# Hybrid SSD/attention/mLSTM/MoE block on one core: two parameter queues, a reordered first norm, and modulation columns by narrow matmuls

## The reference

```python
h = rmsnorm(x, norm_mix) * (1 + scale) + shift
x = x + gate * mixer(h)
h = rmsnorm(x, norm_ffn) * (1 + scale_f) + shift_f
x = x + gate_f * moe(h)
```

## Time and profile before

| | |
|---|---|
| median of 3 runs | 1325.04 us (1325.0 to 1326.84) |
| the profiled execution's own time | 1311.33 us |
| its span | 1309.5 us |
| TensorE busy | 1105.2 us, 84% |
| VectorE, ScalarE, GpSimd busy | 39%, 19%, 17% |
| mean granted TensorE clock | 0.912 of full speed |

### The profile page before, as it was taken

One profiled execution on the slowest core, in us unless ns is written; L12 is line 12 of the kernel. 1 busy time (PEld: TensorE's weight loads), 2 busy tenths in 40 slices (PEclk: granted clock), 3 DMA queues, 4 the chain that ended last, 5 costly groups with the idle time before them and its releaser, 6 DMA issues.

```text
span 1309.5 us, 13521 instructions
## 1 busy us (share of the span) xinstructions
PE 1105.2 (84%) x5097; PEld 576.4 (44%) x5097; DVE 510.6 (39%) x1004; ACT 249.0 (19%) x481; POOL 224.4 (17%) x218
## 2 busy tenths in 40 slices
PE   3899978799899479999999199998868489869992
PEld 0445444443454434444455164445544355434441
DVE  0434656655501522221222678326461433322213
ACT  2222121365511400000001332111010301000001
POOL 0001031000011063333211302000001174332001
PEclk8899978899999789999999599999668789999997
DMA  9732155779161359999995832122007279999982
GB/s 354 224 106 89 66 192 193 249 260 392 63 257 67 130 197 408 409 416 415 347 400 231 330 124 69 64 102 92 1 0 321 100 270 411 413 416 417 425 333 111
DMA packets 74366, 309.79 MB, mean 237 GB/s; under 512 B 11789, under 2 KB 14013, under 8 KB 57131
## 3 DMA queue, kind: packets, MB, share of 16 engines
q1 hardware_dynamic: 63947, 292.70, 57.4%
q0 software_dynamic: 9472, 12.77, 2.8%
q10 hardware_dynamic: 864, 3.15, 0.6%
HBM read 308.41 MB, written 15.34 MB: 247 GB/s over the span
## 4 chain that ended last, share of the span: by engine, by line
PE 70%; DMA 10%; DVE 10%; ACT 3%; issue 3%; SPq 3%; POOL 1%; ACTq 0%; POOLq 0%; DVEq 0%
PE psum L1828 9%; DMA arena<-in_moe_w 9%; PE psum L1831 9%; PE psum L1196 7%; PE psum L1101 6%; PE psum L1863 5%; PE psum L551 5%; PE psum L1858 4%; PE psum L543 3%; PE psum L1209 2%; PE psum L377 2%; SPq L2023 2%; PE psum L996 2%; PE psum L1447 1%; PE psum L838 1%
## 5 line engine op out<-in xcount | busy, mean ns | idle before, releaser
L1944 POOL DMA_INDIRECT arena<-hdram,idxl x128 | 128.7, 1005 | 258.1 <-DVE arena L1903 168.7
L1918 DVE TENSOR_TENSOR arena<-arena,psum 128x512 f32<-128x512 f32 x32 | 22.0, 687 | 271.7 <-PE psum L1828 142.4
L1196 PE MATMUL psum<-arena,ring 128*128 128x512 f32 (+1 forms) x256 | 97.8, 540 | 0.0
L1828 PE MATMUL psum<-arena 128*64 128x256 f32 x736 | 82.8, 381 | 8.8 <-DMA arena<-in_moe_w 7.4
L1831 PE MATMUL psum<-ring,arena 128*128 128x512 f32 x176 | 78.9, 606 | 10.6 <-DVE arena L1903 9.8
L1828 PE MATMUL psum<-ring,arena 128*64 128x256 f32 x672 | 77.7, 389 | 11.6 <-DVE arena L1903 9.2
L1101 PE MATMUL psum<-ring,arena 128*128 128x512 f32 x192 | 82.9, 593 | 1.5 <-ACT arena L1086 1.5
L1125 POOL TENSOR_TENSOR xres<-xres,arena 128x512 f32<-128x512 f32 x12 | 15.2, 1262 | 384.2 <-DVE arena L1114 384.2
L1886 ACT ACTIVATE arena<-psum 128x512 f32<-128x512 f32 x32 | 19.1, 597 | 281.7 <-PE psum L1858 173.7
L1903 DVE STREAM_TRANSPOSE arena<-arena 128x1024 f32<-128x1024 f32 x32 | 64.9, 2029 | 18.3 <-DMA arena<-hdram,idxl 18.3
L551 PE MATMUL psum<-ring,arena 128*128 128x512 f32 (+1 forms) x192 | 69.0, 522 | 0.0
(11 more groups left out here) (369 smaller groups left out, 1572.6 us busy)
## 6 DMA issues: line engine op xcount, KB each, us to landing
ring<-in_moe_w SPq DMA_DIRECT2D x48, 2048.0 KB, 14.4
arena<-in_moe_w SPq DMA_DIRECT2D x48, 2048.0 KB, 15.5
ring<-in_w_mod SPq DMA_DIRECT2D x24, 2048.0 KB, 8.9
ring<-in_od_w_in SPq DMA_DIRECT2D x6, 2048.0 KB, 11.3
ring<-in_ev_w_in SPq DMA_DIRECT2D x3, 2048.0 KB, 9.2
arena<-ydram SPq DMA_DIRECT2D x6, 1024.0 KB, 6.9
ring<-in_ev_w_out SPq DMA_DIRECT2D x2, 2048.0 KB, 12.5
ring<-in_od_w_out SPq DMA_DIRECT2D x2, 2048.0 KB, 7.7
```

The costliest lines, as they stand in the source:

```text
L1196: mm = pe.matmul(bank(bk, tok.stop - tok.start), w[:, k, P * (b % 4):P * (b % 4) + P], hT[:, k, tok], start=k == 0, stop=k == KD - 1)
L1828: mm = pe.matmul(psum[64 * g:64 * g + 64, hbank(e, j), 0:256], xT[b][:, k, 0:64], w[:, k, 256 * g:256 * g + 256], start=k == 0, stop=k == ...
L1944: pool.indirect_dma_start(xq[e % NX][:, 256 * g:256 * g + 256], None, xrows(l), bass.IndirectOffsetOnAxis(ap=idxl[:, g, e:e + 1], axis=0), ...
```

## The change

Seven parameters (convolution weights and biases, norm weights, `b_mod`) stay in SyncE's queue. The other 17 (`LATER`) are issued by GpSimd once the memory is cleared and chunk 1's rows are done; a second semaphore counts them. The steps that need them, `act_setup_rest` and a new `dve_setup_later`, are moved behind the xBC evacuations and convolutions. The first half of the first norm's transposes is put ahead of chunk 3 in TensorE's program. Chunk columns are made by a float32 matmul with a 128x2 selector, `streamsel`, which transposes, picks and sums in one; the result is 8 columns in bank 7, copied by VectorE, and the next chunk's rows wait for that copy. In the rounds for long lists TensorE's four semaphores become one.

```diff
+    streamsel = cf[:, 618:620]
...
     PARAMS = [
-        (cb[:, :], const_b),
         (r3[0:18, :], ev_conv_w[0].rearrange("t (b n) -> (t b) n", n=P)),
...
         (brow[0:2 * MODC, :], b_mod.rearrange("l (c n) -> (l c) n", n=512)),
+    ]
+    LATER = [
+        (cb[:, :], const_b),
         (rw32[:, :, 0:E], router_w.rearrange("(k p) e -> p k e", p=P)),
...
-            PARAMS.append((rowpar[r:r + H, j:j + 1], w[0, d].unsqueeze(1)))
+            LATER.append((rowpar[r:r + H, j:j + 1], w[0, d].unsqueeze(1)))
...
     def act_setup_rest():
-        act.wait_ge(S("params"), PARAMS_IN)
+        act.wait_ge(S("later"), LATER_IN)
...
         dve.wait_ge(*dve_more("cols_ready"))
+
+    def dve_setup_later():
+        dve.wait_ge(S("later"), LATER_IN)
         dve.wait_ge(*dve_more("c_exp"))
...
     def pe_mod_rows(m):
+        if m > 0:
+            pe.wait_ge(S("mcol_done"), m)
         weights_here(mod_pos(m))
...
     def pe_mod_cols(m):
         pe.wait_ge(*pe_more("modrow_ready"))
-        if m > 0:
-            pe.wait_ge(*pe_more("mcol_done"))
         for b in range(4):
-            mm = pe.transpose(psum[:, 6, P * b:P * b + P], modrow[:, P * b:P * b + P], ident)
+            mm = pe.matmul(psum[:, 7, 2 * b:2 * b + 2], modrow[:, P * b:P * b + P], streamsel, start=True, stop=True)
...
-        dve.tensor_reduce(mcol[:, l, 4 * ch:4 * ch + 4, :],
-                          bank(6).rearrange("p (b g r) -> p b r g", b=4, g=4)[:, :, 0:2, :], AX.X, ALU.add
-                          ).then_inc(S("mcol_done"), 1)
+        dve.tensor_copy(mcol[:, l, 4 * ch:4 * ch + 4, :], bank(7, 8).rearrange("p (b r) -> p b r", b=4)
+                        ).then_inc(S("mcol_done"), 1)
...
     def pe_norm(tiles):
-        pe.wait_ge(*pe_more("xn_ready", len(tiles)))
-        for k in range(KD):
+        pe_norm_blocks(tiles, range(4))
+        pe_norm_blocks(tiles, range(4, KD))
+
+    def pe_norm_blocks(tiles, blocks):
+        if blocks[0] == 0:
+            pe.wait_ge(*pe_more("xn_ready", len(tiles)))
+        for k in blocks:
...
     def pe_router(l, tiles):
-        pe.wait_ge(S("params"), PARAMS_IN)
+        pe.wait_ge(S("later"), LATER_IN)
...
+    def pool_later():
+        pool.wait_ge(S("zeroed"), 1)
+        pool.wait_ge(S("mod_full"), 2)
+        for dst, src in LATER:
+            pool.dma_start(dst, src).then_inc(S("later"), 16)
...
         def _(eng):
+            pool_later()
             pool.wait_ge(S("in_full"), 4)
...
             act_mod(3)
-            act_setup_rest()
             act_norm_rows(0, 0, ALL)
             act.wait_ge(*act_more("raw_cleared"))
             act_in_even("xbc")
+            act_setup_rest()
             act_conv()
...
             dve_mod(2)
+            dve_setup_rest()
             dve_mod(3)
-            dve_setup_rest()
...
-            for m in range(FIRST):
+            for m in range(FIRST - 1):
                 pe_mod(m)
             pe_setup_rest()
-            pe_norm(ALL)
+            pe_norm_blocks(ALL, range(4))
+            pe_mod(FIRST - 1)
+            pe_norm_blocks(ALL, range(4, KD))
             pe_in_even()
...
+    f[:, 618:620] = np.arange(P)[:, None] % DIR1 == np.arange(2)
```

More of the change, by code:

```diff
@@ L316, in hybrid_program @@
             r = DIR1 * d + (2 * DIR1 if w is od_fgate_b else 0)
-            PARAMS.append((rowpar[r:r + H, j:j + 1], w[0, d].unsqueeze(1)))
+            LATER.append((rowpar[r:r + H, j:j + 1], w[0, d].unsqueeze(1)))
     PARAMS_IN = 16 * len(PARAMS)
+    LATER_IN = 16 * len(LATER)
     def act_setup():
@@ L509, in pe_norm @@
             mm.then_inc(S("ht_full"), 1)
-        pe.wait_ge(*pe_more("ht_act", 2))
-        pe.wait_ge(*pe_more("ht_dve", 2))
+        if blocks[0] > 0:
+            pe.wait_ge(*pe_more("ht_act", 2))
+            pe.wait_ge(*pe_more("ht_dve", 2))
     EV0 = FIRST
@@ L593, in dve_in_even @@
                      colsa[:, 66 + b:67 + b])
+        dve_setup_later()
         dve.wait_ge(S("in_full"), 7)
@@ L2056, in body @@
         def body(r, e, n):
-            turn, last = sp.to_reg(n + 6), sp.to_reg(n + 1)
+            turn, last = sp.to_reg(n + 6), sp.to_reg(n * 4 + 4)
             sp.wait_ge(S("rows_ready"), l + 1)
@@ L2064, in body @@
             sp.wait_ge(S("rows_ready"), l + 1)
-            sp.wait_ge(extra(l, "y"), last)
+            sp.wait_ge(extra(l, "pe"), last)
         extra_rounds(sp, l, tiles, body, ahead)
@@ L2093, in body @@
                                   xq[0].rearrange("p (n k) -> p k n", k=KD)[:, k, :], ident)
-            mm.then_inc(extra(l, "xt"), 1)
+            mm.then_inc(extra(l, "pe"), 1)
             pe.wait_ge(extra(l, "w"), n * 48 + 48)
@@ L2100, in body @@
                     mm = pe.matmul(bank(j), xT[0][:, k, :], w[:, k, :], start=k == 0, stop=k == KD - 1)
-            mm.then_inc(extra(l, "h"), 1)
+            mm.then_inc(extra(l, "pe"), 1)
             pe.wait_ge(extra(l, "a"), n + 1)
@@ L2104, in body @@
                 mm = pe.transpose(psum[:, 6, P * k:P * k + P], ah_block(ah[0], k, False), ident)
-            mm.then_inc(extra(l, "at"), 1)
+            mm.then_inc(extra(l, "pe"), 1)
             pe.wait_ge(extra(l, "atout"), n + 1)
@@ L2110, in body @@
                     mm = pe.matmul(bank(2 + half), aT[0][:, k, :], w[:, k, 512 * half:512 * half + 512], start=k == 0, stop=k == KF - 1)
-            mm.then_inc(extra(l, "y"), 1)
+            mm.then_inc(extra(l, "pe"), 1)
         extra_rounds(pe, l, tiles, body, lambda: pe_drained(l))
@@ L2119, in body @@
         def body(r, e, n):
-            act.wait_ge(extra(l, "xt"), n + 1)
+            act.wait_ge(extra(l, "pe"), n * 4 + 1)
             act.activation(flat(xT[0][:, 0:4, :]), bank(4), ACT.Copy)
             act.activation(flat(xT[0][:, 4:8, :]), bank(5), ACT.Copy).then_inc(extra(l, "xtout"), 1)
-            act.wait_ge(extra(l, "h"), n + 1)
+            act.wait_ge(extra(l, "pe"), n * 4 + 2)
             act.activation(ah[0], bank(0), ACT.Silu).then_inc(extra(l, "sil"), 1)
@@ L2130, in body @@
             dve.tensor_tensor(ah[0], ah[0], bank(1), ALU.mult).then_inc(extra(l, "a"), 1)
-            dve.wait_ge(extra(l, "at"), n + 1)
+            dve.wait_ge(extra(l, "pe"), n * 4 + 3)
             dve.tensor_copy(flat(aT[0]), bank(6)).then_inc(extra(l, "atout"), 1)
-            dve.wait_ge(extra(l, "y"), n + 1)
+            dve.wait_ge(extra(l, "pe"), n * 4 + 4)
             dve.tensor_copy(yb[0][:, 0:512], bank(2))
@@ L2348, in constants @@
 def constants():
-    f = np.zeros((P, 618), np.float32)
+    f = np.zeros((P, 620), np.float32)
+    f[:, 618:620] = np.arange(P)[:, None] % DIR1 == np.arange(2)
     f[:, 602:618] = np.where(np.tri(4, k=-1), -2e-38, np.where(np.eye(4), 1e30, 0.0)).reshape(1, 16)
```

## The result

| | before | changed |
|---|---|---|
| median | 1325.02 us (1324.19 to 1326.84, 4 runs) | 1349.88 us (1343.62 to 1350.72, 4 runs) |
| ratio | | 1.0188 (1.0151 to 1.0224) |
| profiled execution, span | 1311.33, 1309.5 | 1350.45, 1348.6 |

The change is 1.9% slower. Measured again beside later experiments (`after_again`) it is 1.0149 (1.0111 to 1.0188). The first profiled execution of the kernel before was quicker than any of its other executions (1311.33 against 1318 and more), so the two spans differ by 39 us, and the medians by 25. A mark is the start of the first instruction of its kind in the trace.

The account below looks back on a forecast made before the run. The prediction took TensorE to hold 70% of the chain of waits. It summed tokens 1.7, start order 0.0 and columns 5.6 to +7.3 us, taking the median from 1325.0 to 1332.3, range 1324 to 1338.

Parts of the forecast that it names:

- The columns, 5.6: Scan phase, the chunk after it and attention: two-column matmuls replacing four transposes a chunk add 5.6 us.
- I take 0.87, the nearest row: Chunk columns on TensorE: eight passes take 0.87 us at the higher clock, from the 16 passes of L838 in 1.74.
- the wait before the rows: Chunk rows waiting for the last chunk's columns: about 1 lost between chunks 0 and 1, inside the token wait; elsewhere 0.
- The parameters, 0: Moved parameters and their consumers: the 1.48 us parameter wait goes, later consumers are absorbed at cost 0.
- the tokens, 1.7: Start: GpSimd's `cb` transfer, 648 KB at 394 GB/s, makes the tokens 1.7 us later; bounds 0 and 4.0.
- should land just behind chunk 3, before TensorE asks for them: Start: the seven parameters left in SyncE's queue land at about 32 to 34, so TensorE's wait of 1.48 goes.
- The order, 0.0: Start: hiding transposes and unpacking trades evenly against chunk 3 wholly behind VectorE's scaling; 0.5 earlier to 3.1 later, taken 0.0.
- the half microsecond of low clock: Start, from scaled rows to first evacuation: TensorE at the higher clock except for half a microsecond at the lower.
- What comes after, 0: A microsecond won or lost up to the end of attention was priced as one at the end.
- (a): Chunk columns on TensorE: cheap two-column passes or one load and pass make the kernel faster, 1321.0 us; chance 0.10.
- (b): Attention and scan: the columns' extra time falls into waits for VectorE and ScalarE, no change, 1326.1 us; chance 0.20.
- (c): Start: late parameters ahead of the tokens, lower clock through chunk 3, the seven late too: 1337.7 us; chance 0.12.

Follow-up runs that it names:

- cols_only: Kernel before with only the chunk columns changed to the two-column float32 matmul, bank 7, rows waiting for the copy: 1338.29 us, ratio 1.0093.
- ht_new_cols: Old order, 17 parameters by GpSimd after the first four norm blocks, plus new columns and the wait before each chunk's rows: 1337.84 us, ratio 1.0100 to before.
- after_old_cols: Changed kernel with the four transposes into bank 6, the reduction and the place of the wait put back: 1323.47 us, ratio 1.0000 to before.
- params_tokens: Changed kernel with old columns and old order; GpSimd's 17 parameter transfers start when the tokens have landed: 1319.78 us, ratio 0.9947 to before.
- params_ht: As params_tokens, but GpSimd's transfers start when the first four norm blocks are transposed: 1318.55 us, ratio 0.9934 to before.
- ht_new_order: As params_ht, but first half of the norm's transposes and the parameter transposes ahead of chunk 3: 1323.77 us, ratio 0.9988 to before.
- second profile of before: Kernel before, unedited, profiled a second time: span 1324.9 us; its runs 1325.94 us, ratio 1.0014.
- old_cols_later_tokens: Changed kernel with old columns and GpSimd's transfers started only when the tokens have landed: 1326.35 us, ratio 0.9990 to before.

## Why the prediction was wrong

The sign was right, and so was the cause of the largest term. The forecast was +7.3, with a range to 1338; the time was 1349.9. Three terms were mis-sized (the columns, the parameters, the low clock in the start), and one stood at nothing without a reason: what the lower clock takes behind the start.

**The columns, 5.6.** They cost 12.3 alone, 10.7 of it by the end of attention. The step that failed is "I take 0.87, the nearest row": the pace of sixteen passes in a full stream was taken for eight behind a wait. They took 1.05 in the scan phase, so the difference to the transposes was 0.39 there and not 0.22, and 0.79 to 0.98 in attention, where TensorE comes to them without a wait, 0.40 a step and not 0.31. The bound of 0.98 that I drew from the earlier trace rows was too low too. Two things stood at nothing. One is the 0.11 that L838 loses behind them in each scan step. The other is the wait before the rows in the old order of the start, where I wrote that VectorE is done elsewhere: the copy of chunk 2 comes after the scaling in VectorE's program, and chunk 3's rows waited 1.51 in `cols_only`. That was to be read from the order of the calls; in the changed kernel, with its new order, the step held. The three attention chunks that I counted by half, at 0.15, lost 0.10 each, so that step held as well.

From the first projection to the end of attention, the stretch that I had 5 to 6 us longer, the columns made it 8.4 longer in `ht_new_cols` (322.9 against 314.5) and 8.0 in `cols_only` (325.6 against 317.5), with 3 to 4 us more at the lower clock. The changed kernel took 330.1, against 314.6 in `after_old_cols`: 15.5, with 62 us at the lower clock against 38. So some 7 us are left that the columns alone don't explain. They go with the clock, and what sets its pattern stays open.

**The parameters, 0, and the tokens, 1.7.** The tokens were late by 2.4 in the changed kernel and by 3.4 in `after_old_cols`, between my bounds of 0 and 4.0. That two queues take turns, as the Trainium skill's "DMA: Bandwidth & Descriptors" has it (Queues, rings and completion order), agrees with the trace: with GpSimd's start moved behind the tokens they came at 26.3 again. A strict order by age doesn't. A queue of GpSimd's that always went first isn't excluded, since all its bytes would take up to 4.0. But the same bytes also delayed the seven: the step "should land just behind chunk 3, before TensorE asks for them" failed: TensorE waited 2.47 us. And moving the parameters is worth more than I gave it. Where nothing delays the tokens it is 7 to 9 us, as `params_tokens` and `params_ht` show, 3.2 to 3.7 of it at the first projection: the wait goes, the widening of 1.1 us goes from ahead of the first evacuation, and TensorE, working on without a gap, is at the higher clock in the norm's transposes.

**The order, 0.0.** It costs 0.4 to 0.5%. `ht_new_order` shows it in the first projection, 2.5 late, where my sum at the higher clock had it 0.5 early. The step that failed is the half microsecond of low clock: in the changed kernel the transposes at 41.09 take 3.64, which is the lower clock all through. The reason I named, chunk 3 wholly behind the scaling, is the one that holds. My two zeros, for the parameters and the order, were nearly right as a sum: with both and nothing else (`ht_new_order`) the first projection is at 48.2, against 48.1 and 48.9 in the two profiles of before. But that was a gain of 3.2 and a loss of 2.5: the order hides a wait and an unpacking that moving the parameters had already taken off the path.

**What comes after, 0.** I priced a microsecond won or lost up to the end of attention as one at the end. For the changed kernel nothing was regained, and 17.8 became 23.7: 2.0 came in the projections, with 4 us of them at the lower clock, and 5.9 after attention, where 195 us ran at the lower clock against 181.5 in the second profile of before. So the price was too low. And what I wrote of the start, that hardly anything lost there can be caught up, fails with the old columns: 3.5 us late at the first projection became 0.6 at the end of attention (`after_old_cols`), and 4.0 between two versions became 1.1 (`old_cols_later_tokens`).

**Rivals.** (a) is out: the group costs 1.05, and with 64 columns only 0.05 more. The Trainium skill's 60 cycles for a short lone pass ("TensorE: Matmul & The Clock Gate", Back-to-back issue gap) would make it 0.2 us for the eight, as an estimate; the measurement decides against that for passes that each bring their own float32 weights. (b), hidden columns, is out by `cols_only`. (c) was nearest for the start, which lost 5.3 by its causes, late tokens, late parameters and a low clock, but it had the columns at 5.6, and its 1337.7 lies 12 under the measured time. By its own sum the chance that I gave to slower is 0.74, not 0.72.

## What to carry to other kernels

A transpose of float32 data is one weight load and one pass for each 128x128 block, while a float32 matmul on the same block is two of each, however few columns it moves: count passes with their loads, not columns, and price a short group behind a wait by a short group behind a wait. A second queue of transfers shares the bandwidth with whatever the first has under way, so start it when the transfer that the path waits for has landed; with the old columns and the old order that brought the first projection from 50.1 to 45.2. In the time it is the step from 0.4% gained to 0.5 or 0.7%, which the intervals don't tell apart. An order of work that hides a wait is worth nothing once the wait is gone, and may then cost: measure such a pair one by one. A wait that is free in steady state must be checked once at each place where its producer's program has something long in front.

## What the runs showed that I had not expected

Eight passes with two columns took 1.05 us and with 64 columns 1.10, in the same place. One execution of a kernel was 14 us quicker than its median, 7 us of it by one wait in unchanged code, so a single profile is a weak base for a sum of a few microseconds. And the kernel's tail, in code that is the same, took from 955 us with 175 us at the lower clock to 965 with 199 (the first profile of before was 10 shorter still): versions whose first projections are 4 apart can come out equal, and two that differ by 12 at the end of attention can come out 20 apart.
